# Feed-forward down projections with one 512-column matmul for both activation halves

## The reference, cut to what matters

```
x = x + conv_ffn(rmsnorm(x, norm2_w), ffn_up, ffn_conv_w, ffn_down)

def conv_ffn(h, w_up, conv_w, w_down):
    up = h @ w_up
    gate, val = split(up, 2)
    gate = causal_dwconv(gate, conv_w)
    return (gelu(gate) * val) @ w_down        # the down projection
```

## Time and profile before

| | |
|---|---|
| time, median of 3 runs | 3365.55 us (3365.45 to 3366.45) |
| span of the profiled execution, first to last instruction | 3364.8 us |
| PE busy | 3322.3 us (99%), 27834 matmuls |
| DVE busy | 2191.7 us (65%) |
| ACT busy | 1711.6 us (51%) |
| POOL busy | 309.8 us (9%) |
| DMA | 584.28 MB, mean 174 GB/s |
| mean granted TensorE clock | 0.997 of full speed |

### The profile page before, as it was taken

How to read it: one execution, slowest core, us unless ns; L and a number is a source line. 1 busy time by engine, 2 the same in 40 slices (tenths; PEclk the granted TensorE clock), 3 DMA queues, 4 the chain that set the end, 5 groups by cost and what they waited for, 6 DMA issues and landing times. The chain is left out here.

```text
span 3364.8 us, 72970 instructions
## 1 busy us (share of the span) xinstructions
PE 3322.3 (99%) x27834; PEld 3282.9 (98%) x27834; DVE 2191.7 (65%) x3584; ACT 1711.6 (51%) x2803; POOL 309.8 (9%) x314
## 2 busy tenths in 40 slices
PE   8999999999999999999999999999999999999999
PEld 7999999999999998899999999999899999999999
DVE  7667666656656666678755665665778755666655
ACT  5555644434434455656544554444665654554443
POOL 1010100000000025011002200001012101210000
PEclk9999999999999999999999999999999999999999
DMA  5234555555555554444455545555444455445554
GB/s 190 107 112 148 176 186 189 189 186 187 188 187 187 187 187 159 139 163 158 161 197 184 183 161 188 188 201 177 146 153 163 156 178 209 172 162 188 187 206 162
DMA packets 90629, 584.28 MB, mean 174 GB/s; under 512 B 10480, under 2 KB 11120, under 8 KB 28400
## 3 DMA queue, kind: packets, MB, share of 16 engines
q1 hardware_dynamic: 88992, 577.47, 48.7%
q0 software_dynamic: 1488, 4.72, 0.4%
HBM read 580.05 MB, written 2.10 MB: 173 GB/s over the span
## 5 line engine op out<-in xcount | busy, mean ns | idle before, releaser
L172 DVE TENSOR_TENSOR w_lo<-raw,w_hi 128x768 fp32r<-128x768 f32 (+5 forms) x1202 | 1378.5, 1159 | 372.6 <-ACT w_hi L161 365.6
L191 PE MATMUL bank<-h,w_hi 128*128 128x256 f32 x5168 | 1459.3, 282 | 16.5 <-DVE w_lo L172 12.0
L161 ACT ACTIVATE w_hi<-raw 128x768 fp32r<-128x768 f32 (+4 forms) x1190 | 1095.7, 968 | 692.3 <-PE bank L193 615.4
L193 PE MATMUL bank<-h,w_lo 128*128 128x256 f32 x5168 | 1444.1, 279 | 0.0
L192 PE MATMUL bank<-h,w_hi 128*128 128x256 f32 x5168 | 1443.6, 279 | 0.0
L191 PEld LDWEIGHTS bank<-h,w_hi 128*128 128x128 f32 x5168 | 973.1, 188 | 22.0 <-DVE w_lo L172 10.2
L192 PEld LDWEIGHTS bank<-h,w_hi 128*128 128x128 f32 x5168 | 973.2, 188 | 2.6 <-issue 1.9
L193 PEld LDWEIGHTS bank<-h,w_lo 128*128 128x128 f32 x5168 | 972.8, 188 | 0.0
L191 PE MATMUL bank<-mixed,w_hi 128*128 128x256 f32 x2272 | 634.9, 279 | 0.7 <-DVE w_lo L172 0.7
L193 PE MATMUL bank<-mixed,w_lo 128*128 128x256 f32 x2272 | 634.5, 279 | 0.0
L192 PE MATMUL bank<-mixed,w_hi 128*128 128x256 f32 x2272 | 633.8, 279 | 0.0
(11 more groups left out here) (408 smaller groups left out, 3340.4 us busy)
## 6 DMA issues: line engine op xcount, KB each, us to landing
raw<-in_w SPq DMA_DIRECT2D x485, 1024.0 KB, 4.8
raw<-in_w_br SPq DMA_DIRECT2D x96, 512.0 KB, 3.8
raw<-in_w_uq SPq DMA_DIRECT2D x8, 768.0 KB, 4.4
raw<-in_w_ukv SPq DMA_DIRECT2D x8, 512.0 KB, 3.3
bias_t<-in_bias POOLq DMA_DIRECT2D x16, 192.0 KB, 4.2
x<-in_x SPq DMA_DIRECT2D x4, 512.0 KB, 7.7
raw<-in_w_kr SPq DMA_DIRECT2D x4, 512.0 KB, 3.3
out_x<-x SPq DMA_DIRECT2D x3, 512.0 KB, 7.5
```

The costliest lines, as they stand in the source:

```text
L161: act.activation(w_hi[:, b % 2, c], raw[:, b, c], ACT.Copy).then_inc(S["hi_done"], 1)
L172: dve.tensor_tensor(w_lo[:, b % 2, c], raw[:, b, c], w_hi[:, b % 2, c].bitcast(F32), ALU.subtract).then_inc(S["lo_done"], 1)
L191: pe.matmul(o, w_hi[:, b % 2, c], a_hi, start=start and k == t0, stop=False)
L193: last = pe.matmul(o, w_lo[:, b % 2, c], a_hi, start=False, stop=stop and k == t0 + nt - 1)
```

## The change

The down units of all three thirds take a new function. The matmuls of w_hi with the upper and with the lower activation half become one matmul over all 512 columns of the `mixed` tile, into all 512 columns of the bank. w_lo x a_hi adds into columns 0 to 255 as before. At the last k the order of the two is swapped. A bank so holds two partial sums, and DVE adds both to x, one after the other, with a wait on a new semaphore `x_part` between them. The semaphore on which PE, ACT and `gained_lo` wait is raised by the second add. The up units, the output projection before the feed-forward network and the hybrid layers keep `unit`.

```
+        def wide_tiles(pe, n, b, buf, o, k0, k1, ready=None):
+            for k in range(k0, k1):
+                if k in (0, first_tiles(KT)):
+                    pe.wait_ge(S["lo_done"], 8 * n + 2 * b + (1 if k == 0 else 2))
+                if ready is not None:
+                    ready(k)
+                c = slice(k * P, (k + 1) * P)
+                if k < KT - 1:
+                    pe.matmul(o[:, :], w_hi[:, b % 2, c], buf[:, k, :], start=k == 0, stop=False)
+                last = pe.matmul(o[:, 0:SEQ], w_lo[:, b % 2, c], buf[:, k, 0:SEQ], start=False, stop=False)
+                if k == KT - 1:
+                    last = pe.matmul(o[:, :], w_hi[:, b % 2, c], buf[:, k, :], start=False, stop=True)
+            if k1 == KT:
+                last.then_inc(S["unit_done"], 1)
...
-                        dve.tensor_tensor(x[:, ft, :], x[:, ft, :], bank[b % 2][:, 0:SEQ].unsqueeze(1), ALU.add).then_inc(S[f"x_add{b % 2}"], 1)
+                        dve.tensor_tensor(x[:, ft, :], x[:, ft, :], bank[b % 2][:, 0:SEQ].unsqueeze(1), ALU.add).then_inc(S["x_part"], 1)
+                        dve.wait_ge(S["x_part"], third * KT + 4 * i + b + 1)
+                        dve.tensor_tensor(x[:, ft, :], x[:, ft, :], bank[b % 2][:, SEQ:2 * SEQ].unsqueeze(1), ALU.add).then_inc(S[f"x_add{b % 2}"], 1)
...
-                    unit(pe, n, b, of(mixed), [(bank[b % 2][:, 0:SEQ], 0, KT, True, True)],
-                         products(third) if third is not None and b == 0 else None)
+                    if wide:
+                        wide_tiles(pe, n, b, mixed, bank[b % 2], 0, KT, products(third) if third is not None and b == 0 else None)
+                    else:
+                        unit(pe, n, b, of(mixed), [(bank[b % 2][:, 0:SEQ], 0, KT, True, True)])
...
-                        unit(pe, n0 + 8 + i, b, of(mixed), [(bank[b % 2][:, 0:SEQ], 0, KT, True, True)],
-                             products(third) if first and b == 0 else None)
+                        wide_tiles(pe, n0 + 8 + i, b, mixed, bank[b % 2], 0, KT, products(third) if first and b == 0 else None)
```

More of the change, by code:

```diff
@@ L285, in first_block @@
     sb, at_least, first_tiles = g["sb"], g["at_least"], g["first_tiles"]
-    load_unit, split_hi, split_hi_part, split_lo, split_lo_part, unit, unit_tiles, of = (
-        g[k] for k in ("load_unit", "split_hi", "split_hi_part", "split_lo", "split_lo_part", "unit", "unit_tiles", "of"))
+    load_unit, split_hi, split_hi_part, split_lo, split_lo_part, unit, unit_tiles, wide_tiles, of = (
+        g[k] for k in ("load_unit", "split_hi", "split_hi_part", "split_lo", "split_lo_part", "unit", "unit_tiles",
+                       "wide_tiles", "of"))
     x, h, ident, ones, eps = (g[k] for k in ("x", "h", "ident", "ones", "eps"))
@@ L1410, in _, with way_out @@
                 blocks(i)
-            def way_out(n, i, added, third=None, b0=0):
+            def way_out(n, i, added, third=None, b0=0, wide=False):
                 for b in range(b0, 4):
@@ L1465, in ffn_third @@
                 if last:
-                    way_out(n0 + 8, 0, KT // 2 + third * (KT // 2), third)
+                    way_out(n0 + 8, 0, KT // 2 + third * (KT // 2), third, wide=True)
                     with pe.Fori(1, 4) as i:
-                        way_out(n0 + 8 + i, i, KT // 2 + third * (KT // 2))
+                        way_out(n0 + 8 + i, i, KT // 2 + third * (KT // 2), wide=True)
                     sum_squares(pe, 1, 2 * SEQ)
```

## The result

The changed kernel takes 3373.93 us (median of 20 runs, 3371.07 to 3376.63), the kernel before 3367.33 us (median of 20, 3365.45 to 3369.63). The ratio is 1.002, 95% interval 1.0014 to 1.0026: +6.6 us, slower by just about 0.2%. The prediction said 3369.5 us, range 3364.5 to 3373.5, most likely no change. The direction of its sum was right (+4.0), the size too small, and 3373.93 lies outside, 0.4 us above the upper end.

The account below looks back on a forecast made before the run. PE was taken as the bound, with a serial loop nearly filling its unit in the last third. Terms -1.7 + 5.2 - 0.1 + 0.57 = +4.0 us gave span 3368.8, with 0.75 offset 3369.5 us; range 3364.5 to 3373.5.

Parts of the forecast that it names:

- Part 1: PE's stream, down units of the first two thirds: fusing saves 3.3 ns per k, -1.7 us (ends -2.7 and +0.9).
- Part 2: DVE's second add in the first two thirds: 0.57 us each, hidden in 2.19 us of idle time, priced at nothing.
- Part 3: Last third: second add lengthens the serial DVE-ACT loop from 5.38 to 5.97 us, +5.2 us (ends 4.9 and 7.6).
- Part 4: Tail after the last unit: second add delays ACT's squares and the barrier, +0.57 us, end 0.68.
- Part 5: Clock and transfers: half-clock stretch behind the barrier may change; taken as 0, allowed -1.2 to +0.5 us.
- The offset: Whole kernel: 0.75 us, by which the median lay above the span before, added to the forecast span of 3368.8 us.
- A: Second add hidden in the last third too, since the loop has misread slack; 3363.6 us, chance 0.10.
- B: Last third's loop longer, from a gap between adds of 0.26 us or more; 6.25 us gives 3373.5, chance 0.13.
- C: A 512-column matmul costs as one of 256, each k dropping from 350 to 233 ns; about 3313 us, chance 0.02.
- D: Fusion saves a fixed 10 ns on each removed matmul, -5.1 instead of -1.7 us; 3366.1 us, chance 0.05.

Follow-up runs that it names:

- experiment 1: Changed kernel but with three narrow 256-column matmuls per k, both adds kept; 3371.13 us, ratio 1.0013 to the kernel before.
- experiment 2: Wide matmuls and two adds only in the first two thirds, last third as in the kernel before; 3369.52 us, ratio 1.0009 to it.
- experiment 3: Wide matmuls and two adds only in the last third, the rest as in the kernel before; 3370.42 us, ratio 1.0012 to it.
- experiment 4: The changed kernel run and profiled again, nothing altered; 3373.06 us, ratio 1.002 to the kernel before.
- experiment 6: Changed kernel plus one small fp32 matmul ahead of the up units of the second and third third; 3371.27 us, ratio 1.0012 to the kernel before.
- experiment 7: Changed kernel with the last third reordered: ACT and DVE finish tile b-1 behind the split of b+1; 3369.05 us, ratio 1.0007 to the kernel before.
- experiment 10: The kernel before with only the last third's order of ACT and DVE work changed; 3366.76 us, ratio 1.0000 to the kernel before.
- experiment 5: Changed kernel with the very last down unit of the first and second third narrow (three 256-column matmuls per k); one run, 3370.71 us.
- experiment 8: Changed kernel with both the small fp32 matmul ahead of the up units and the reordered last third; 3366.20 us, ratio 0.9998 to the kernel before.
- experiment 9: Wide matmuls only in the first two thirds, plus the small fp32 matmul ahead of later up units; 3365.56 us, ratio 0.9998 to the kernel before.

## Why the prediction was wrong

**Part 1, PE's stream: right in mechanism, sized too large, and it missed what comes behind.** It gave 3.3 ns for each k; a unit went from 5.600 to 5.567 us, 2.1 ns. That is -1.0 us in place of -1.7. The step that failed is the one it did not contain, a cost put at nothing without a reason: that the stream of unchanged matmuls behind a changed one keeps its pace. It priced only the units that change ("the up units keep `unit`") and took 116.7 ns as the cost of a 256-column matmul. The trace of before had both rhythms in view. In its hybrid layers, between 1275 and 1800 us, 51 of 328 groups of twelve successive 256-column matmuls run at 117.8 ns and 211 at 116.7 (each within 0.4 ns), and I read only the mean. Experiments 1 to 4 tie the up units' rhythm to the 512-column matmuls ahead of them, experiment 6 shows that it is a state. It is worth +3.3 us, half of the whole loss. The Trainium skill ("TensorE: Matmul & The Clock Gate", Back-to-back issue gap) says that the spacing in a stream of loads and matmuls is set by both together; what decides between two spacings for the same pair, no run here shows.

**Part 2, first two thirds: right.** 2.15 us of idle time remain on DVE in each unit.

**Part 3, the loop: right in place and mechanism, the term mis-sized.** The forecast was 5.38 + 0.57 and a little. The 5.38 us hold to the hundredth: 5.82 - 0.44. The second add costs 0.44 us (1192.02 - 1191.58), not 0.57. L1193 was the wrong neighbour, because DVE computes an address between the two instructions: its trace has a register instruction there, which starts after the first one's end; here none starts behind the first one's end, and the second add starts 0.035 us after the first has ended. In the first two thirds the step is 0.455 us. That makes +3.2 us in place of +5.2. PE's waiting of "0.3 to 0.5 us per unit from the third or fourth unit on" came out as 0.3 us, ten times, from the seventh unit on: the loop overruns PE's unit by 0.26 us, not by 0.42, so the slack lasts longer.

**Part 4, the tail: +0.45 us** in place of 0.57, by the same error.

**Part 5, the clock.** The half-clock stretch was to cost between -1.2 and +0.5 us. In the changed kernel's profile it cost +1.5, in its second profile nothing. Over the profiles here it was 3.4, 6.8 or 10.2 us long, and the range of +0.5 us left no room for the last. The length of the stretch from the last add to the end does not follow from it alone: with 3.4 us it was 2101.9 and 2103.1 (experiments 7 and 10), with 6.8 us from 2102.7 to 2105.5 (experiments 5 and 8), with 10.2 us 2104.95 and 2106.8 (the profile after, experiment 3). Most of the rest is again the rhythm. Behind the first 28 us of that stretch, 114 of 1363 groups of twelve matmuls run at the slow pace in experiment 7 and 362 in experiment 3, and the way to the end takes 2076.1 and 2079.0 us. As an estimate, 248 groups x 12 x 1.11 ns make 3.3 us of these 2.9. Whether the longer standstill of PE before it (2.42 us of waiting in place of 0.90) makes the long stretch more frequent is open; two of ten profiles with changed down units had it, neither of the two without them.

**The offset.** The 0.75 us between span and time was read from a median of other runs. Where both are given for one run, they lie 1.6 to 1.7 us apart (3371.13 against 3369.5 in experiment 1). And the three times shown lay 1.8 us under the median of twenty. That alone moves the measured time out of the range: counted from the median that the forecast started from, the range was -1.1 to +7.9 us, and the change measured is +6.6. The range was also drawn narrower than the prediction's own ends, which reach +9.7 us.

**Luck.** The +4.0 us stood as near to +6.6 as it did because errors cancelled: the second add was put 2.0 us too high in the loop, the gain 0.7 us too high, and the 3.3 us of the rhythm were missing.

**The rivals.** A, the hidden second add, fell with the loop of 5.82 us. B, a longer loop, fell too, although its time (3373.5) came close: the kernel got there by another way. C and D, a real gain from the width, fell with 2.1 ns a k. The Trainium skill's figure of about 131 ns for a 512-column matmul in a stream ("TensorE: Matmul & The Clock Gate", Back-to-back issue gap) does not hold here; the trace has 228 to 235 ns, and the measurement decides. The true cause of half the loss was on nobody's list.

Sum by the trace, with a half-clock stretch of the same length: -1.0 + 3.3 + 3.2 + 0.45 = +6.0 us; measured +6.6 (interval 4.7 to 8.8).

## What to carry to other kernels

Before adding an instruction to an engine that "has time", look for the loop in which it stands: engine after engine, each waiting for the one before, with shares of 60% everywhere and no slack at all. Find out how long that loop is without the bounding engine; here 5.38 us under a unit of 5.60 said that 0.22 us were free and 0.44 not. And where PE runs without a gap, compare the pace of the unchanged matmuls behind the edit too, not only that of the edited ones: here 1% lost on 64 unchanged units outweighed 0.6% gained on 32 changed ones.

## What the runs showed of the hardware

- An uninterrupted stream of fp32r loads and matmuls of 256 columns was seen at two steady paces at full clock, 116.7 and 117.8 ns, with steps that repeat as 120-113-116-118 and 118-119-116 ns. Behind the stream of alternating 512- and 256-column matmuls it was the slower one in all ten such up stretches without a break (the changed kernel twice, experiments 2, 5 and 7), and in the six with a small fp32 matmul between (experiments 6, 8 and 9) the faster one. The pace held over 1536 matmuls. In the long streams of the hybrid layers it differed between two runs of one kernel (experiment 4). What inside PE decides it stays open; it was not tried which other instruction would do.
- A 512-column fp32r matmul in the wide stream steps 228 to 235 ns, as in the earlier trace rows: twice the columns for twice the time. Fusing two of 256 columns into it saves 2.1 ns of the 350 ns of one k.
- Two dependent fp32 adds of 256 columns on DVE, the second waiting for the first on a semaphore, start 0.44 to 0.46 us apart, of which 0.41 to 0.42 are the first one's length. With a register instruction between, it was 0.64 and 0.75 us for an operation of 0.48.
- The same `gained_lo` takes 0.48 us alone, 1.0 us and, in experiment 7, 1.5 us where POOL works on its 512-column sum; that it is POOL's doing was inferred from the times, not tested.
